# One projection stage in split one-pass products, and a top-k selection by a search over the bits of the threshold

## The reference, cut to what matters

```python
hn = rmsnorm(x, g_mix)
parts = split_proj(jnp.einsum('btd,dn->btn', hn, w_in))   # 3656 columns; d = 1024
# sb, df, ds: q, k, v of 256 columns each; indexer: 8 queries of 64, one key of 64, 8 weights;
# fx: q, k, v of 256 columns each and 4 forget gates
```

```python
s_ix = jax.nn.relu(jnp.einsum('bqhd,bkd->bqhk', q_ix, k_ix) * (IDX_DIM ** -0.5))
score = jnp.einsum('bqh,bqhk->bqk', w_ix * (N_IDX_HEADS ** -0.5), s_ix)
score = jnp.where(chunk_ok, score, -jnp.inf)
top_val, top_idx = lax.top_k(score, topk)     # topk: 256 for the prompt, 40 for the sample
```

## Time and profile before

| | us |
|---|---|
| median of 3 runs | 3880.66 (3869.41 to 3881.22) |
| the profiled execution, its own time | 3867.68 |
| its span, first to last instruction | 3865.9 |
| TensorE busy, of the span | 3574.3 (92%) |
| VectorE busy | 2486.4 (64%) |
| ScalarE busy | 1065.8 (28%) |
| GpSimd busy | 34.4 (1%) |
| mean granted TensorE clock | 0.958 of full speed |

### The profile page before, as it was taken

How to read it: one execution, slowest core, us unless ns; L and a number is a source line. 1 busy time by engine, 2 the same in 40 slices (tenths; PEclk the granted TensorE clock), 3 DMA queues, 4 the chain that set the end, 5 groups by cost and what they waited for, 6 DMA issues and landing times. The chain is left out here.

```text
span 3865.9 us, 53489 instructions
## 1 busy us (share of the span) xinstructions
PE 3574.3 (92%) x19553; PEld 2728.9 (71%) x19553; DVE 2486.4 (64%) x4584; ACT 1065.8 (28%) x2223; POOL 34.4 (1%) x160
## 2 busy tenths in 40 slices
PE   3999999999979999999969999989899799999995
PEld 2554555655659999999935555555566699999994
DVE  3188996575754666656635899947655566665665
ACT  3111211565632111111111111245654311111112
POOL 0000000000000000000000000000000000000000
PEclk7999999998989999999989999999999899999997
DMA  4212213211002111111011112141100111111101
GB/s 165 71 37 68 68 38 110 69 57 50 21 12 61 49 49 34 47 49 49 12 63 56 65 41 73 41 145 61 48 12 23 44 50 49 33 48 49 49 28 46
DMA packets 216658, 206.69 MB, mean 53 GB/s; under 512 B 23846, under 2 KB 193158, under 8 KB 214430
## 3 DMA queue, kind: packets, MB, share of 16 engines
q1 hardware_dynamic: 216478, 204.36, 16.4%
HBM read 159.41 MB, written 44.91 MB: 53 GB/s over the span
## 5 line engine op out<-in xcount | busy, mean ns | idle before, releaser
L1624 PE MATMUL psum<-h_split,gate_up_split 128*128 128x352 f32 x6336 | 1019.2, 322 | 44.1 <-DVE gate_up_split L1738 44.1
L1624 PEld LDWEIGHTS psum<-h_split,gate_up_split 128*128 128x128 f32 x6336 | 1011.2, 188 | 48.3 <-issue 46.8
L883 PE MATMUL psum<-arena 128*128 128x512 f32 (+4 forms) x2304 | 756.9, 487 | 0.0
L1768 DVE TENSOR_TENSOR arena<-arena,psum 128x352 f32<-128x352 f32 x1056 | 513.6, 521 | 318.3 <-PE psum L1624 318.2
L883 PEld LDWEIGHTS psum<-arena 128*128 128x128 f32 (+1 forms) x2304 | 413.5, 181 | 329.8 <-issue 291.3
L1624 PE MATMUL psum<-hid_split,down_split 128*128 128x352 f32 x3168 | 523.1, 325 | 11.1 <-DVE down_split L1738 11.1
L1624 PEld LDWEIGHTS psum<-hid_split,down_split 128*128 128x128 f32 x3168 | 516.6, 190 | 11.6 <-issue 11.6
L1022 DVE MAX8 top<-arena 128x8 f32<-128x384 f32 (+6 forms) x394 | 346.6, 880 | 13.5
L1023 DVE MATCH_REPLACE8 arena<-top,arena 128x384 f32<-128x384 f32 (+6 forms) x394 | 339.1, 861 | 0.0
L1496 DVE CUSTOM_DVE_ANT_0 arena<-psum,arena 128x128 f32<-128x128 f32 (+8 forms) x288 | 198.0, 703 | 200.6 <-PE psum L1259 89.9
L1709 ACT CAST hid_split<-hidden 128x1056 fp32r<-128x1056 f32 x44 | 47.3, 1076 | 834.5 <-DVE hidden L1753 834.5
(11 more groups left out here) (139 smaller groups left out, 2677.9 us busy)
## 6 DMA issues: line engine op xcount, KB each, us to landing
gate_up_raw<-in_w_gate SPq DMA_DIRECT2D x44, 512.0 KB, 3.6
gate_up_raw<-in_w_up SPq DMA_DIRECT2D x44, 512.0 KB, 4.7
down_raw<-in_w_down SPq DMA_DIRECT2D x44, 512.0 KB, 3.5
arena<-in_w_in SPq DMA_DIRECT2D x24, 768.0 KB, 7.0
arena<-k_turned SPq DMA_DIRECT2D x8, 1184.0 KB, 5.6
k_turned<-arena SPq DMA_DIRECT2D x72, 128.0 KB, 2.2
q_turned<-arena SPq DMA_DIRECT2D x64, 128.0 KB, 2.1
arena<-bias_strips SPq DMA_DIRECT2D x4, 2048.0 KB, 10.0
```

Source lines behind the costliest of these rows:

```text
L883: ins = nc.tensor.matmul(m.ps[0:n, o + n0:o + n1], m.hT[:, c, c0:c0 + n], w[:, c, n0:n1], start=(c == 0), stop=(c == KC - 1))
L1624: ins = nc.tensor.matmul(out, w[i], x[k], start=(first and n == 0), stop=(last and n == 2))
L1768: nc.vector.tensor_tensor(x, x, bank(m, down_bank[p])[:, 0:PIECE], ALU.add).then_inc(s.added, 1)
```

## The change: what it does

- `stage_norm` ahead of the projections runs with `split=True`.
- The two projection stages become one, `stage_project`. W_in comes in 15 pieces: one "special" piece of 128 columns (index key, index weights, forget gates, padding), two of index queries, and q, k, v of each group, 256 columns each. One raw piece is in SBUF at a time, and two pieces in split form. ScalarE makes the high part of a piece (`high`), GpSimd the low part; SyncE loads the next piece once both are done.
- Special, index and q pieces are computed feature-major: weights stationary, 352 tokens moving, 24 passes for an output of 128 by 352. Those of k and v are token-major: 128 tokens stationary, 256 columns moving, 24 passes. So q and the index queries need no transpose; k does, 80 transposes a layer, and the special piece 10 with the cached index keys.
- The scores use 64 rows of the array, the halves in turn by head; a block's units run through all heads for the first 512 keys and then for the rest. `RELU_RING` is 4.
- The selection searches the threshold of each row bit by bit: 31 times, a comparison of all scores that also counts, and two operations on one value a row. Exact ties are settled by a scan. The masks are 0 and 1; the identity in the attention is scaled by 1e30. The masks of all blocks but the last go by DMA to their place; the last selection waits until every projection output is done (`proj_done`), since its mask lies over the region of the split input.
- A new `ProjectPlan` orders the work by estimates of its own.

```diff
+def block_time(blk):
+    return 31 * (blk.keys / 1300 + 0.55) + 8 * (blk.keys / 960 + 0.2) + 2 * NIX * (blk.keys / 960 + 0.1) * 0.7
...
+            if o.o == self.first_out(p):
+                plan.append(("piece", o.piece))
...
+                    due = max(due, now) + block_time(blk)
+                    if waiting and now >= due - 8:
+                        self.begin(waiting[0])
...
+            plan.append(("out", o))
+            now += 3.75 if o.piece.kind not in "kv" else 2.8
+            if o.piece.kind == "k" and o.i > 0:
+                self.turn(self.outs[o.o - 1])
...
         @block.sync
...
+                if what == "piece" and x.i + 1 < len(pieces):
+                    p = x.i + 1
+                    sp.wait_ge(s.high, p)
+                    sp.wait_ge(s.low, p)
+                    load_piece(m, a, l, pieces[p])(sp, s.raw_in)
...
+            for i, blk in enumerate(SELECTED[:-1]):
+                sp.wait_ge(s.selected, i + 1)
+                dst = m.mix[0:blk.rows, MIX["fx"], 0:blk.keys] if blk.n == NT else taken_keys(m)[blk.n].bitcast(F32)
+                sp.dma_start(dst, rows[blk.n][0:blk.rows, :]).then_inc(s.taken_out, 16)
...
         @block.tensor
...
+                if o.o >= OUT_RING:
+                    pe.wait_ge(s.kept, o.o - OUT_RING + 1)
+                if o.o == plan.first_out(pc.i):
+                    pe.wait_ge(s.high, pc.i + 1)
+                    pe.wait_ge(s.low, pc.i + 1)
...
                 for c in range(KC):
+                    for n, (i, k) in enumerate(((0, 0), (0, 1), (1, 0))):
+                        start, stop = c == 0 and n == 0, c == KC - 1 and n == 2
+                        if pc.kind in "kv":
+                            ins = nc.tensor.matmul(dst[:, 0:GW], m.h_split[:, k, c, t0:t0 + P], w[i][:, c, :], start=start, stop=stop)
+                        else:
+                            ins = nc.tensor.matmul(dst[:, 0:PIECE], w[i][:, c, o.f * P:(o.f + 1) * P],
+                                                   m.h_split[:, k, c, o.c0:o.c0 + PIECE], start=start, stop=stop)
...
         @block.scalar
...
+            def high(p):
+                n = KC * pieces[p].width
+                if p:
+                    act.wait_ge(s.raw_in, raw_count(p))
+                if p >= 2:
+                    act.wait_ge(s.proj_done, plan.last_out[p - 2] + 1)
+                nc.scalar.copy(m.w_split[p % 2][:, 0, 0:n], m.w_raw[:, 0:n]).then_inc(s.high, 1)
+            def piece(pc):
+                if pc.i + 1 < len(pieces):
+                    high(pc.i + 1)
...
         @block.gpsimd
...
+            for pc in pieces:
+                pool.wait_ge(s.high, pc.i + 1)
+                nc.gpsimd.tensor_tensor(w[:, 1, 0:n], m.w_raw[:, 0:n], w[:, 0, 0:n].bitcast(F32), ALU.subtract).then_inc(s.low, 1)
...
         @block.vector
...
+                def counted(out, op, scalar):
+                    own(nc.vector.tensor_scalar(out, score, scalar, None, op, ALU.add, accum_out=count))
+                counted(u, ALU.is_ge, 0.0)
...
+                for bit in range(30, -1, -1):
+                    counted(u, ALU.is_lt, cand)
+                    own(nc.vector.tensor_scalar(step_bits, count, limit, float(1 << bit), ALU.is_ge, ALU.mult))
+                    own(nc.vector.scalar_tensor_tensor(out=cand_bits, in0=step_bits, scalar=(1 << bit) >> 1, in1=cand_bits,
+                                                       op0=ALU.bitwise_xor, op1=ALU.bitwise_xor))
+                own(nc.vector.tensor_scalar(score, score, sign, None, ALU.mult))
...
+                counted(u, ALU.is_le, kth)
+                own(nc.vector.tensor_scalar(v, score, kth, None, ALU.is_equal))
...
+                own(nc.vector.tensor_tensor_scan(out=score, data0=m.ones[0:n, 0:1].to_broadcast([n, keys]), data1=v,
+                                                 initial=0.0, op0=ALU.mult, op1=ALU.add))
+                own(nc.vector.scalar_tensor_tensor(out=score, in0=score, scalar=limit, in1=v, op0=ALU.is_le, op1=ALU.mult))
+                nc.vector.scalar_tensor_tensor(out=flags, in0=score, scalar=-1.0, in1=u, op0=ALU.mult, op1=ALU.add
+                                               ).then_inc(s.selected, 1)
...
-                for _ in range((TOPK_PROMPT if blk.n < NT else TOPK_SAMPLE) // ROUNDS_OF_8):
-                    own(nc.vector.max(m.top[0:blk.rows, :], score))
-                    own(nc.vector.match_replace(out=score, in_to_replace=m.top[0:blk.rows, :], in_values=score,
-                                                imm_value=TAKEN))
-                out = rows[blk.n] if blk.n == NT else taken[blk.n]
-                own(nc.vector.tensor_scalar(out[0:blk.rows, :], score, TAKEN / 2, BIG, ALU.is_gt, ALU.mult))
+                flags = score
+                if blk is SELECTED[-1]:
+                    dve.wait_ge(s.proj_done, len(proj))
+                    flags = taken_keys(m)[blk.n]
+                select(blk, score, flags)
...
-        stage_norm(nc, m, 2 * FC, load_w_in(m, a, l, "ix", 0), params=(a, l))
-        stage_project_index(nc, m, a, l, load_w_in(m, a, l, GROUP_ORDER[0], 1))
-        stage_project_select(nc, m, a, l, d, outs, caches, load_group("ds", 0, l))
+        stage_norm(nc, m, 2 * FC, load_piece(m, a, l, PROJECT.pieces[0]), split=True, params=(a, l))
+        stage_project(nc, m, a, l, d, outs, caches, load_group("ds", 0, l))
```

More of the change, by code:

```diff
@@ L26 @@
 Unit = namedtuple("Unit", "v st heads map0 last")
+Piece = namedtuple("Piece", "i kind of width columns")
+Out = namedtuple("Out", "o piece f i c0 n tau")
+Turned = namedtuple("Turned", "i of out tile c0 n")
 Turn = namedtuple("Turn", "i kind of a t0 tiles eng nth")
@@ new lines, in begin, with turn @@
+    def begin(self, blk):
+        us = []
+        for k0 in range(0, blk.keys, BANK):
+            for h in range(NIX):
+                us.append((self.n_units, h, k0, min(k0 + BANK, blk.keys)))
+                self.n_units += 1
+        self.units[blk.n] = us
+        self.plan.append(("score", (blk, 0)))
+    def turn(self, o, g=None):
+        if o is None:
+            t = Turned(len(self.turns), g, None, NT + 1, 0, P)
+        else:
+            t = Turned(len(self.turns), o.piece.of, o, o.i, o.c0, o.n)
+        self.turns.append(t)
+        self.plan.append(("turn", t))
@@ L972, in _ @@
             act.preload_act_table_set("natural_log_exp_and_others")
-            for what, x in plan:
+            high(0)
+            for what, x in plan.plan:
                 if what != "gates":
-                    {"tile": tile, "turn": turn, "score": score}[what](x)
+                    {"piece": piece, "out": out, "turn": turn, "score": score}[what](x)
         @block.gpsimd
@@ L1134, in stage_attend @@
     steps, units = plan.steps, plan.units
-    taken, rows = taken_keys(m), taken_rows(m)
+    taken = taken_keys(m)
     mask_of = dict(fx=0, sb=1)
```

566 lines of the change are left out of this document (279 added, 287 removed).

## The result

The changed kernel takes **3906.31 us** (median of 5 runs, 3899.91 to 3907.9), the kernel before in the same comparison 3870.52 (5 runs, 3868.16 to 3881.22): ratio **1.0079 [1.0059, 1.0099]**. The forecast was 3835 us, faster. The profiled execution spans 3905.4 us.

A forecast was written before the change was run, and what follows sets the result against it. TensorE sets the stage's end, selection beside it. TensorE 483 us, bare selection 49 and 5 to the attention make 537 a layer against 572; less 12 for the norm, 23 saved, 46 in all: 3835 us, range 3790 to 3905.

The forecast's parts named there:

- second rival: Projection of k and v: a 256-column pass costs 0.161 us, 71 us more a layer, 3977 us; chance 0.1.
- Products: Projection: 358 us a layer of products, 101 less than before; low clock after TensorE's waits adds 17 us.
- The norm: Split norm ahead of the projections: 24 low parts added on VectorE, +12 us a layer.
- the bare tail: Last block's selection waits for the projection's end, so its whole 49 us stands bare with TensorE idle.
- ScalarE's standing: ScalarE stands 8.5 us at each piece's start ahead of the copies; TensorE's waits for it come to 32 us.
- A pass that also counts: Selection's counting pass: taken at 0.52 ns a column like the plain comparison, with 1.05 as the other end.
- the rival: First rival: counting pass runs one column a cycle, last selection grows 18 us; 3871 to 3899, about 3885; chance 0.17.
- the prediction's formula: Selection time from counting passes, small operations and closing passes: 29 to 49 us a block, 278 for seven blocks.
- the 560: Sign of being wrong: projection to attention takes more than 560 us a layer.
- The 91 us left: VectorE between first and last scores: 376 us available, 285 needed, the rest idle, 10 to 25 before most blocks.
- Scores: 52 us: Score products with 64 rows in turn, two beside each other: 52 us for 88 units, 84 before.
- a case of its own: Third rival: stalls, low clock and half-height products not overlapping cost all the gain; about 3875 us; chance 0.15.

The follow-up runs named there:

- the best run: Changed kernel with small blocks by rounds, one-input exclusive or, late projection wait, new plan estimates, and ScalarE's cast behind the third output's copy: 3742.84 us, 0.9652 to before.

## Why the prediction was wrong

**What held.** A pass of 256 columns: 0.128 us with its half-clock stretches, 0.12 forecast (second rival out). Products: 380 us a layer with their share of the low clock, where I had 358 and 17. The norm: from the MLP's end to the norm's end 48.1 us for 38.5, +9.6 for my +12. The low part by GpSimd, which had no row: 4.58 us, inside my bounds, 1 us above the value taken. The place and cause of the bare tail, and ScalarE's standing ahead of the copies at the piece starts: right, and TensorE's waits outside the scores came to 20 us a layer, under my 32 and 5 for the gates.

**The step that failed first: "A pass that also counts has no row. Ends: 0.52 ns, or 1.05 ... I take 0.52, since it is the same operation".** It is 1.04. I had both ends and took the wrong one: the plain comparison was the nearest row by name, not by what it does. The bare stretch, selection with handoff, is 69.2 for 54: +15 a layer, where the rival said 18. The passes of all blocks cost 386.8 us in place of 257.1 (with and without the count), 65 a layer. With GpSimd's hold, the seven selections come to 379.5 us a layer where the prediction's formula has 278; the rounds took 375. So there was nothing saved that could have lain beside TensorE's work, and projection to attention took 574.6 us, past the 560 at which the prediction called itself wrong.

**The second: "The 91 us left are idle time of VectorE, 10 to 25 us before most blocks".** From the first adds to the last there are 410 us; between a selection's last counting pass and the next block's adds lie 2.8 to 5.2 us, most of it the selection's own last operations, and 9.5 once, at the gates. The dear passes took the slack, and GpSimd's hold took 42 us a layer (18 exclusive ors and four first adds, 84 us above their usual length in both layers), as the rival had it (43). What of that comes through is less: 11 us a layer for the counting, by the run without it, and 8 for the long exclusive ors.

**The third, and the largest: "Scores: 52 us".** They cost 64 us busy and 30 idle, 94. A unit keeps TensorE busy 0.73 us (127.9/176; 0.85 before), so the two halves of the array save a seventh and not the third that 52 needs. The waits are for relus, from a ScalarE that stands at a piece's start or, later, from a full VectorE. No run separates what bounds a unit's 0.73 us. So TensorE's end is 505 for 483: scores +42, products and clock +5, transposes +4, waits elsewhere 15 to 20 less, and some 10 to 15 of this are overlaps between groups that a sum of busy times counts twice.

**The attention** got 14 us longer, which I had at nothing. The windows from its first product to the MLP's first, both layers of the kernel before:

```profile
666.60:1168.50 501.90, 448.82 (x3097) 285.04 (x3097) 309.36 (x729) 263.09 (x648) 0.24 (x2) 0.92 0.13 43
2549.30:3039.60 490.30, 436.84 (x3096) 278.10 (x3097) 309.08 (x729) 262.99 (x648) 0.23 (x2) 0.95 0.14 44
```

and of the changed one:

```profile
678.90:1183.80 504.90, 451.79 (x3096) 287.10 (x3096) 309.50 (x729) 263.33 (x648) 0.24 (x2) 0.91 0.13 43
2577.00:3078.00 501.00, 448.37 (x3096) 285.22 (x3096) 309.50 (x729) 263.26 (x648) 0.23 (x2) 0.92 0.13 43
```

The same work takes 490 us at a granted clock of 0.95 or some 502 at 0.92, in kernels of every kind (490.6 in one layer of the run without the count and of the best run, about 502 in the other). The kernel before had one of each in this execution, and its runs lie between 3867 and 3885. A part of the 14 us is this and no effect of the change; the 69 us of idle ahead of the attention aren't needed for the longer value, since the kernels with 25 us there have 501 to 506 us too, in all but one layer. What sets the two values stays open.

**Together**, from profile to profile: forecast -46, measured +39.5, a gap of 85. Bare tail 2 x 15, TensorE's end 2 x 22, norm 2 x -2.4, attention 14: 83. The range missed by 1 us, since it stopped at the first rival's far end: the rival came true with all its parts, and the scores' shortfall, which I had only as a case of its own, came on top of it. The rival's own sum has a slip as well: 58 + 43 - 91 is 10 us a layer, not 14, so its far end was 3891 and not 3899, and the 3905 of the range comes from neither.

## What to carry to other kernels

Price an instruction by what it does, not by its name: a comparison that also accumulates ran at half the rate of the plain one here, and when both ends are in hand, the forecast should be weighed by what the rest depends on. Where a queue serves several consumers, look what waits in it: a cast that waits 7 us for a load, put three outputs later, was worth 56 us, almost as much as the whole count (63). Work placed earlier is worth something only up to the next floor, and an in-order engine pays at once for scores whose consumer isn't ready.

## What the runs showed that I had not expected

- The accumulating form (shown as TENSOR_SCALAR_CACHE_REDUCE): 1280 ns for 1024 columns, 754 without the count, and 83 ns more for the read of the count.
- During GpSimd's low part VectorE's counting passes and one-input operations of one value run on unhindered, and so do MAX8 and MATCH_REPLACE8 (some 95 of them began during a low part in the run with rounds, none longer than 1.1 us), while an operation of 160 ns with two SBUF inputs, or a plain comparison, ends up to 4.6 and 5.1 us after its start. The accumulating pass, slower by itself, was never held in any of these traces, so taking the count out of it gives less than its rows say.
- The search costs the same whatever the number sought (30 us for the 160 keys of the sample, against 4 for five rounds), and at 384 keys, where nothing holds it, it is not faster than 32 rounds (40.5 and 40.4 us). At 1024 it is 66 against 83.
